# A hybrid encoder step on one core: order of the attention blocks, place of the search's state and of the MLP's low halves

## The chip, the cores and the metric

The kernel runs on one core of one Trainium2 chip. The metric is the device time of one execution in microseconds (us), lower is better. An execution of the profiler is read beside it; its span runs from the first to the last profiled instruction.

## The reference, cut to what matters

One inference step of a two-layer encoder on 1024 prompt frames and 32 sample frames, model width 1024, everything in float32. Layer 0 joins stick-breaking attention and a spatial-gating MLP. Layer 1 joins the attention below with a short gated convolution. After each mixer comes an MLP of width 4096, the same for both layers.

```python
def dsa_attend(q, qi, wi, q_pos, k, v, ki, k_pos, top_k):
    qk_idx = einsum('bqhe,bke->bqhk', qi, ki) * (D_IDX ** -0.5)
    score = einsum('bqhk,bqh->bqk', relu(qk_idx), wi) * (H_IDX ** -0.5)      # 4 index heads
    admissible = (k_pos[None, :] // CHUNK) <= (q_pos[:, None] // CHUNK)      # CHUNK = 64
    score = where(admissible, score, NEG)
    _, idx = lax.top_k(score, top_k)                                         # 256 keys, sample 136
    ...
    p = softmax(logits)                                                      # over the selected keys alone
    ...

def sq_relu_ffn(h, w1, w2):
    return jnp.square(jax.nn.relu(h @ w1)) @ w2
```

## The kernel before, in words

Activations lie transposed: features on the 128 partitions, the 1056 frames (1024 and 32) along the free dimension. Every float32 product with weights is made from three products of high and low parts (`gemm_tile`, L246 to L261): an output tile of 128 features by 1056 frames is 3 column pieces of 352 in three PSUM banks, and the jobs alternate between two such sets (banks 0 to 2 and 3 to 5, `psz`). A job waits until its set was evacuated (`set_free`) and reports on `job_done`. POOL splits each block of weights into high and low (`split`, L1676 and L1680) while PE works on the block before; SP's queue loads them.

**The MLP** (`pe_ffn`, `act_ffn`, `dve_ffn`, L274 to L357) has 16 chunks of 256 hidden features. For one chunk PE makes two up tiles (72 matmuls each, eight input tiles) and eight down tiles (18 matmuls each), and it makes the up tiles of chunk c+1 ahead of the down tiles of chunk c. For an up tile DVE evacuates with relu and scale into `rbuf` (L336), ACT squares (L316) and copies the rounded high half to `hid` (L318), DVE then makes the low half (L339) and counts `hid_ready`. For a down tile DVE adds the PSUM set to the residual `xT` (L347). DVE's order is: first tile's L336 and L339, second tile's L336 and L339, eight times L347.

**Index scores** (PE L1096 to L1112, ACT L1226 to L1233, DVE L1301 to L1316). Query blocks 2 to 7 and the sample, four index heads each, make 28 rounds. PE writes a round's scores, up to 1024 columns, into one of four pairs of banks; ACT applies relu and copies it to one of two SBUF tiles `rl`; DVE multiplies by the head's weight `wi` and accumulates in the SBUF tile `score` (L1309 for the first head, L1312 for the others). PE waits for the relu of four rounds ago, ACT for the accumulation of two rounds ago. After the 28th relu PE begins the 16 tiles of the first eight projection units of layer 1.

**The search** (L1322 to L1351, ACT's `count` L1237). The threshold of the k-th largest score of each row is found bit by bit in 32 rounds. In a round ACT counts the scores of three blocks against the candidate (L1242) and DVE those of the other four (L1340), then DVE works on tiny rows of seven columns in the SBUF tile `bs_`: two candidates for the next round (L1344, L1345), the comparison (L1348), the choice (L1350), which lets ACT go on, and the new threshold (L1351). ACT empties one of the first 12 projection tiles after two or three rounds (L1253). After the search DVE repairs the threshold and makes the mask of the selected keys (L1390 to L1397); ACT's squares of the queries (L1260) wait for that, and PE's sums over them too (L544).

**Attention over the selected keys** (PE L1140 to L1173, ACT L1264 to L1274, DVE L1423 to L1447, POOL L1482 to L1489). 36 steps: block b = step // 4, with b+1 key tiles of 128, and last the sample (b = 8, 544 keys); a step is one pair of heads. PE makes the scores (L1153); DVE scales, masks and takes the extreme (L1438); ACT takes exp with the sum (L1273); DVE the reciprocal (L1428); POOL multiplies (L1487); two steps later PE turns both matrices (L1184) into banks 4 and 5, ACT and DVE copy one each (L1287); three steps later PE multiplies with the values (L1211) into bank 6 or 7, and DVE stores the block (L1446). Beside the first 28 steps POOL runs one instruction of the short convolution each (`conv`, L1463 to L1480). The head of this stretch also has DMAs on SP's queue: copies of keys, stores of keys, values and convolution state, and the next weights.

```python
for n, (a, b) in enumerate(((0, 0), (0, 1), (1, 0))):            # L256, three products
...
ACT_BLOCKS, DVE_BLOCKS = (5, 4, 3), (2, 1, 6, 0)                 # L1064, who counts which block
...
if 0 <= it - 2 < NPAIR:                                          # L1167, PE's order in a step
    pe_p_turns(pe, 2 * (it - 2))
if 0 <= it - 3 < NPAIR:
    pe_pv(pe, it - 3)
if 0 <= it - 2 < NPAIR:
    pe_p_turns(pe, 2 * (it - 2) + 1)
```

## Time and profile before

| what | before |
|---|---|
| median of 3 runs | 2800.72 us (2800.42 to 2802.06) |
| profiled execution | 2799.82 us |
| its span | 2798.1 us |
| mean granted clock of TensorE | 0.973 |
| busy: PE, DVE, ACT, POOL | 2654.0, 1242.0, 667.4, 1166.8 us |

In the profile, PE is TensorE's matmuls and PEld its weight loads, DVE is VectorE, ACT ScalarE, POOL GpSimd, SP the engine whose queue issues most DMAs. L12 is line 12 of the kernel before. PEclk is the granted clock of TensorE as a share of full speed (1.0 is 2.4 GHz, 0.5 is 1.2 GHz). "[0.65 <-DVE xT L347]" behind an instruction says that its engine sat idle for 0.65 us before it, and that L347 on DVE ended the wait. A busy engine is not a bound by itself; what counts is what a wait was for.

### The profile page before, as it was taken

What the parts mean: (1) busy time and instruction counts of PE and PEld (TensorE: products, weight loads), DVE (VectorE), ACT (ScalarE), POOL (GpSimd) and SP (SyncE); (2) the same over time, 40 slices, a digit from 0 to 9 for tenths busy, and PEclk for the clock granted to TensorE, in tenths of its full rate; (3) what the DMA queues carried; (4) which work ended last, traced back from release to release, by engine and by line L of the source; (5) the groups of instructions that cost most, each with busy time, mean ns of one, the idle gap of its engine ahead of it and who ended that gap; (6) DMA issues with size and microseconds to landing.
All of it is one profiled execution on the core that took longest, in us unless ns stands there. A gap on an engine that the chain in (4) does not pass through costs nothing.

```text
span 2798.1 us, 38333 instructions
## 1 busy us (share of the span) xinstructions
PE 2654.0 (95%) x16253; PEld 2448.9 (88%) x16253; DVE 1242.0 (44%) x1575; ACT 667.4 (24%) x926; POOL 1166.8 (42%) x969
## 2 busy tenths in 40 slices
PE   6999999999999999999978996899999999999998
PEld 6998744699999999999965995568999999999998
DVE  5223477634333232323348998464342323232334
ACT  3200378612010101000126751354110000000000
POOL 4332366444333333334433333772433334444441
PEclk8999999999999999999999998799999999999999
DMA  5110300011111111111012110301111111111101
GB/s 189 46 46 32 114 9 1 38 57 45 45 45 45 45 45 45 45 45 45 20 66 69 45 45 15 65 2 63 46 46 45 45 45 45 45 45 45 45 30 63
DMA packets 96239, 134.02 MB, mean 48 GB/s; under 512 B 17393, under 2 KB 81969, under 8 KB 95634
## 3 DMA queue, kind: packets, MB, share of 16 engines
q1 hardware_dynamic: 92466, 114.35, 12.9%
q10 hardware_dynamic: 3680, 18.36, 1.6%
q8 instruction: 67, 1.10, 0.2%
q14 instruction: 26, 0.21, 0.0%
HBM read 113.16 MB, written 18.73 MB: 47 GB/s over the span
## 4 chain that ended last, share of the span: by engine, by line
PE 75%; DVE 12%; ACT 6%; issue 3%; POOL 2%; DMA 1%; another core or an unknown queue 0%; DVEq 0%; ACTq 0%; POOLq 0%
PE PS L259 63%; ACT reach L1242 3%; PE PS L1211 2%; PE PS L1184 2%; DVE xT L347 1%; PE PS L1153 1%; DVE rbuf L336 1%; ACT rbuf L316 1%; ACT hid L318 1%; PE PS L868 1%; PE PS L896 1%; DVE score L1312 1%; POOL spr L1015 1%; DVE reach L1340 1%; DVE sp L971 1%
## 5 line engine op out<-in xcount | busy, mean ns | idle before, releaser
L1676 POOL TENSOR_TENSOR w_sp<-stage,ones 128x512 fp32r<-128x512 f32 x372 | 391.9, 1086 | 1403.7 <-PE PS L259 1363.7
L259 PE MATMUL PS<-h,w_sp 128*128 128x352 f32 (+1 forms) x5256 | 873.4, 326 | 42.8 <-POOL w_sp L1680 14.7
L259 PEld LDWEIGHTS PS<-h,w_sp 128*128 128x128 f32 (+1 forms) x5256 | 856.1, 189 | 51.8 <-issue 25.3
L259 PE MATMUL PS<-hid,w_sp 128*128 128x352 f32 x4608 | 756.4, 324 | 19.6 <-DVE xT L347 19.6
L259 PEld LDWEIGHTS PS<-hid,w_sp 128*128 128x128 f32 x4608 | 743.4, 188 | 28.3 <-DVE xT L347 28.3
L259 PE MATMUL PS<-hz,w_sp 128*128 128x352 f32 x3456 | 567.7, 323 | 0.0
L259 PEld LDWEIGHTS PS<-hz,w_sp 128*128 128x128 f32 x3456 | 558.7, 188 | 0.0
L1680 POOL TENSOR_TENSOR w_sp<-stage,w_sp 128x512 fp32r<-128x512 f32 x372 | 526.5, 1449 | 0.0
L347 DVE TENSOR_TENSOR xT<-PS,xT 128x1056 f32<-128x1056 f32 x256 | 318.8, 1254 | 336.3 <-PE PS L259 336.3
L316 ACT ACTIVATE rbuf<-rbuf 128x1056 f32<-128x1056 f32 x64 | 69.7, 1089 | 1259.3 <-DVE rbuf L336 1259.3
L336 DVE SCALAR_TENSOR_TENSOR rbuf<-PS,rstd 128x1056 f32<-128x1056 f32 x64 | 80.5, 1257 | 505.3 <-PE PS L259 505.3
L339 DVE TENSOR_TENSOR hid<-rbuf,hid 128x1056 fp32r<-128x1056 f32 x64 | 93.5, 1461 | 145.6 <-ACT hid L318 145.6
L1242 ACT ACTIVATE reach<-score,bs__68 128x1024 bf16<-128x1024 f32 (+2 forms) x96 | 99.0, 1033 | 29.0 <-DVE bs__68 L1350 27.5
L771 DVE TENSOR_TENSOR Z<-PS,rstd 128x1056 f32<-128x1056 f32 x20 | 25.1, 1257 | 176.6 <-PE PS L259 176.6
L1015 POOL TENSOR_TENSOR spr<-sp,spr 128x1024 fp32r<-128x1024 f32 (+4 forms) x53 | 91.5, 1727 | 4.4
L1340 DVE TENSOR_SCALAR_CACHE_REDUCE reach<-score,bs__68 128x640 bf16<-128x640 f32 (+3 forms) x128 | 88.6, 745 | 2.0 <-DVE bs__68 L1351 0.4
L1013 POOL TENSOR_SCALAR spr<-sp 128x1024 fp32r<-128x1024 f32 (+4 forms) x53 | 42.0, 793 | 75.2 <-DVE sp L971 64.6
L1487 POOL TENSOR_SCALAR Lb<-Lb,st 128x128 f32<-128x128 f32 (+8 forms) x72 | 52.9, 750 | 45.6 <-DVE st L1428 45.5
L318 ACT ACTIVATE hid<-rbuf 128x1056 fp32r<-128x1056 f32 x64 | 69.6, 1088 | 2.0
L960 DVE SCALAR_TENSOR_TENSOR zs<-PS,zs 128x1024 f32<-128x1024 f32 (+4 forms) x53 | 48.0, 905 | 41.0 <-PE PS L868 40.6
L868 PE MATMUL PS<-spr,tri_r 128*128 128x512 f32 (+4 forms) x212 | 52.4, 372 | 11.0 <-POOL spr L1015 10.7
L1184 PEld LDWEIGHTS PS<-ident,Lb 128*128 128x128 f32 x288 | 31.5, 144 | 32.5 <-issue 26.9
(259 smaller groups left out, 1898.5 us busy)
## 6 DMA issues: line engine op xcount, KB each, us to landing
stage<-in_w_ffn SPq DMA_DIRECT2D x64, 1024.0 KB, 5.1
stage<-in_w_in_odd SPq DMA_DIRECT2D x10, 1024.0 KB, 4.9
stage<-in_w_in_even SPq DMA_DIRECT2D x9, 1024.0 KB, 5.0
x_spill<-xT ACTq DMA_DIRECT2D x2, 4224.0 KB, 14.0
xT<-x_spill ACTq DMA_DIRECT2D x2, 4224.0 KB, 13.5
xtok<-in_x_prompt SPq DMA_DIRECT2D x8, 512.0 KB, 7.7
stage<-in_w_out_even SPq DMA_DIRECT2D x4, 1024.0 KB, 8.9
stage<-in_w_out_odd SPq DMA_DIRECT2D x4, 1024.0 KB, 13.4
```

Source lines behind the costliest of these rows:

```text
L259: mm = pe.matmul(out[0:m, c, :], lhs, rhs(k, b)[:, c * CH:(c + 1) * CH], start=(k == 0 and n == 0), stop=(k == nk - 1 and n == 2))
L316: act.activation(x, x, ACT.Square).then_inc(s_done, 1)
L318: act.activation(hid[:, c % 2, t, 0, :], x, ACT.Copy).then_inc(hhi_done, 1)
L336: dve.scalar_tensor_tensor(tri3(rbuf[:, t, :]), psz(j + t), 0.0, tri3(rstd[:, :]), ALU.max, ALU.mult).then_inc(set_free[(j + t) % 2], 1)
L339: dve.tensor_tensor(hid[:, c % 2, t, 1, :], rbuf[:, t, :], hid[:, c % 2, t, 0, :].bitcast(F32), ALU.subtract).then_inc(hid_ready, 1)
L347: dve.tensor_tensor(tri3(xT[:, m, :]), psz(j + m), tri3(xT[:, m, :]), ALU.add).then_inc(set_free[(j + m) % 2], 1)
L1015: pool.tensor_tensor(lo, x, hi.bitcast(F32), ALU.subtract).then_inc(a_lo, 1)
L1184: mm = pe.transpose(PS[:, 4 + kt // 4, (kt % 4) * P:(kt % 4 + 1) * P], Lb[:, t % 6, kt * P:(kt + 1) * P], ident[:, :])
L1242: act.activation(reach[:, r], score[:, r], ACT.Sign, scale=-1.0, bias=bs_[:, n % 2, bi:bi + 1], accum_out=bs_[:, 2, bi:bi + 1]).then_inc(a ...
L1340: ch.mark(dve.tensor_scalar(reach[0:m, r], score[0:m, r], bs_[0:m, now, bi:bi + 1], 0.0, ALU.is_lt, ALU.add, accum_out=bs_[0:m, CNT, bi:bi ...
L1676: pool.tensor_tensor(w_sp[:, s, 0, q:q + 512], stage[:, s, q:q + 512], ones[:, 0:1].to_broadcast([P, 512]), ALU.mult).then_inc(w_hi_done, 1)
L1680: lo = pool.tensor_tensor(w_sp[:, s, 1, q:q + 512], stage[:, s, q:q + 512], w_sp[:, s, 0, q:q + 512].bitcast(F32), ALU.subtract)
```

## The change

There are four edits.

1. In the MLP, the low half of a chunk's second up tile is no longer made straight after its evacuation but after the first down tile of the chunk before it was added (`low`, `low_of`). The first up tile's low half stays, and so do both of chunk 0.
2. Attention takes its blocks in the order 7, 6, 5, 4, 3, 2, 1, 0, then the sample (`BLOCKS`). The convolution's instructions stay with the step numbers. Banks 6 and 7 go by the place in the order.
3. The index scores' relu is written back into its PSUM banks, and DVE reads them there. `rl` and ACT's wait for DVE are gone; PE waits for the accumulation of four rounds ago, and for the 27th before the projections.
4. In the search, threshold, comparison result and the bound to compare with lie in PSUM bank 7 (`state`); the candidates, UP and the counts stay in `bs_`. From the second round UP is made from the threshold by one xor with two bits. The threshold is copied back once at the end.

```diff
@@ -327,33 +327,38 @@
...
-            def up(c, dj2=0, dj=0, dt=0):
+            def low(c, t, dt=0):
+                dve.wait_ge(hhi_done, c0 + 2 * c + t + 1 + dt)
+                dve.tensor_tensor(hid[:, c % 2, t, 1, :], rbuf[:, t, :], hid[:, c % 2, t, 0, :].bitcast(F32),
+                                  ALU.subtract).then_inc(hid_ready, 1)
+
+            def up(c, dj2=0, dj=0, dt=0, last=True):
                 j = j0 if c == 0 else j0 + 2 + 10 * (c - 1)
                 for t in range(2):
-                    n = c0 + 2 * c + t
                     dve.wait_ge(job_done, j + t + 1 + dj)
...
                                              ALU.mult).then_inc(set_free[(j + t) % 2], 1)
-                    dve.wait_ge(hhi_done, n + 1 + dt)
-                    dve.tensor_tensor(hid[:, c % 2, t, 1, :], rbuf[:, t, :], hid[:, c % 2, t, 0, :].bitcast(F32),
-                                      ALU.subtract).then_inc(hid_ready, 1)
-
-            def down(c, dj2=0, dj=0):
+                    if t == 0 or last:
+                        low(c, t, dt)
+
+            def down(c, dj2=0, dj=0, dt=0, low_of=None):
...
                                       ALU.add).then_inc(set_free[(j + m) % 2], 1)
+                    if m == 0 and low_of is not None:
+                        low(low_of, 1, dt)
...
                 for c in (0, 1):
-                    up(c + 1, dj2=i * 10, dj=i * 20, dt=i * 4)
-                    down(c, dj2=i * 10, dj=i * 20)
-            up(15)
-            down(14)
+                    up(c + 1, dj2=i * 10, dj=i * 20, dt=i * 4, last=False)
+                    down(c, dj2=i * 10, dj=i * 20, dt=i * 4, low_of=c + 1)
+            up(15, last=False)
+            down(14, low_of=15)
             down(15)
@@ -1029,7 +1034,6 @@
...
         zslot = lambda name, s, shape: at(name, o_z + s * ZB, shape)
-        rl = [zslot("rl0", 9, [P, D]), zslot("rl1", 10, [P, D])]
         qiP = zslot("qiP", 16, [P, 4, NT])
@@ -1058,6 +1062,7 @@
...
         NPAIR = 36
+        BLOCKS = [7, 6, 5, 4, 3, 2, 1, 0, 8]
         ROWS = [P] * 6 + [TS]
@@ -1096,7 +1101,7 @@
...
                 if n >= 4:
-                    pe.wait_ge(i_relu, n - 3)
+                    pe.wait_ge(i_acc, n - 3)
                 b0 = 2 * (n % 4)
@@ -1109,7 +1114,7 @@
...
                 mm.then_inc(i_mm, 1)
-            pe.wait_ge(i_relu, 28)
+            pe.wait_ge(i_acc, 27)
             with pe.Fori(0, 4) as i:
@@ -1139,7 +1144,7 @@
...
                 if it < NPAIR:
-                    b, p = it // 4, it % 4
+                    b, p = BLOCKS[it // 4], it % 4
                     g = p // 2
@@ -1175,7 +1180,7 @@
...
-            b, e = t // 8, t % 2
+            b, e = BLOCKS[t // 8], t % 2
             pe.wait_ge(c_n, t + 1)
@@ -1192,12 +1197,12 @@
...
-            b, p = i // 4, i % 4
+            q, b, p = i // 4, BLOCKS[i // 4], i % 4
             g = p // 2
...
                 pe.wait_ge(c_pt[e], i + 1)
-            if p == 0 and b >= 2:
-                pe.wait_ge(c_at, b - 1)
+            if p == 0 and q >= 2:
+                pe.wait_ge(c_at, q - 1)
             n, m = (b + 1, P) if b < 8 else (5, TS)
@@ -1208,7 +1213,7 @@
...
                         w, v = w[0:TS, kt * TS:(kt + 1) * TS], vtc[0:TS, 8, g * HD:(g + 1) * HD]
-                    mm = pe.matmul(PS[64 * e:64 * e + 64, 6 + b % 2, p * P:p * P + m], v, w,
+                    mm = pe.matmul(PS[64 * e:64 * e + 64, 6 + q % 2, p * P:p * P + m], v, w,
                                    start=(kt == 0), stop=(kt == n - 1))
@@ -1226,11 +1231,8 @@
...
                 act.wait_ge(i_mm, n + 1)
-                if n >= 2:
-                    act.wait_ge(i_acc, n - 1)
-                m = ROWS[bi]
-                act.activation(rl[n % 2][0:m, 0:SCN[bi]], banks(2 * (n % 4), SCN[bi], m), ACT.Relu,
-                               scale=HD * HD ** -0.5).then_inc(i_relu, 1)
+                x = banks(2 * (n % 4), SCN[bi], ROWS[bi])
+                act.activation(x, x, ACT.Relu, scale=HD * HD ** -0.5).then_inc(i_relu, 1)
             act.wait_ge(i_acc, 28)
@@ -1265,7 +1267,7 @@
...
                 if it < NPAIR:
-                    m, n = (P, (it // 4 + 1) * P) if it < 32 else (TS, PAST + TS)
+                    m, n = (P, (BLOCKS[it // 4] + 1) * P) if it < 32 else (TS, PAST + TS)
                     for e in range(2):
@@ -1276,7 +1278,7 @@
...
-            b, e = t // 8, t % 2
+            b, e = BLOCKS[t // 8], t % 2
             x = pT[t % 4]
@@ -1303,7 +1305,7 @@
...
                 s = score[0:m, SC0[bi]:SC0[bi] + SCN[bi]]
-                x, w = rl[n % 2][0:m, 0:SCN[bi]], wi[0:m, tile, hh:hh + 1]
+                x, w = banks(2 * (n % 4), SCN[bi], m), wi[0:m, tile, hh:hh + 1]
                 dve.wait_ge(i_relu, n + 1)
@@ -1322,13 +1324,16 @@
...
             u = lambda r, a=0, b=7: bs_[:, r, a:b].bitcast(I32)
+            state = PS[:, 7, 0:64].rearrange("p (r b) -> p r b", b=8)
+            fp = lambda r: state[:, r, 0:7]
+            up_ = lambda r: state[:, r, 0:7].bitcast(I32)
             dve.wait_ge(i_acc, 28)
             ch.mark(dve.memset(f(CNT), 0.0))
-            ch.mark(dve.memset(u(THR), -1))
+            ch.mark(dve.memset(up_(THR), -1))
             for bi in range(7):
...
-                ch.mark(dve.memset(bs_[:, KV, bi:bi + 1], float(n - 2 * k + 1 if bi in ACT_BLOCKS else n - k)))
+                ch.mark(dve.memset(state[:, KV, bi:bi + 1], float(n - 2 * k + 1 if bi in ACT_BLOCKS else n - k)))
             dve.memset(u(0), 0).then_inc(cand_set, 1)
@@ -1341,14 +1346,18 @@
...
                     bit = 1 << (30 - n)
-                    ch.mark(dve.tensor_scalar(u(UP), u(now), bit, None, ALU.bitwise_xor))
-                    ch.mark(dve.tensor_scalar(u(nxt), u(THR), bit, None, ALU.bitwise_xor))
+                    if n == 0:
+                        ch.mark(dve.tensor_scalar(u(UP), u(now), bit, None, ALU.bitwise_xor))
+                    else:
+                        ch.mark(dve.tensor_scalar(u(UP), up_(THR), 3 * bit, None, ALU.bitwise_xor))
+                    ch.mark(dve.tensor_scalar(u(nxt), up_(THR), bit, None, ALU.bitwise_xor))
                 ch.sync()
                 dve.wait_ge(act_count, 3 * n + 3)
-                ch.link(dve.tensor_tensor(u(KEPT), f(CNT), f(KV), ALU.is_le))
+                ch.link(dve.tensor_tensor(up_(KEPT), f(CNT), fp(KV), ALU.is_le))
                 if n < 31:
-                    dve.copy_predicated(u(nxt), u(KEPT), u(UP)).then_inc(cand_set, 1)
-                ch.link(dve.copy_predicated(u(THR), u(KEPT), u(now)))
+                    dve.copy_predicated(u(nxt), up_(KEPT), u(UP)).then_inc(cand_set, 1)
+                ch.link(dve.copy_predicated(up_(THR), up_(KEPT), u(now)))
+            ch.link(dve.tensor_copy(u(THR), up_(THR)))
@@ -1427,7 +1436,7 @@
...
                 if it < NPAIR:
-                    b = it // 4
+                    b = BLOCKS[it // 4]
                     m, n = (P, (b + 1) * P) if b < 8 else (TS, PAST + TS)
@@ -1440,11 +1449,11 @@
...
                 if it >= 7 and it % 4 == 3:
-                    b = it // 4 - 1
-                    c0, m = tok(b)
-                    dve.wait_ge(c_pv, 4 * b + 4)
+                    q = it // 4 - 1
+                    c0, m = tok(BLOCKS[q])
+                    dve.wait_ge(c_pv, 4 * q + 4)
                     dve.tensor_copy(Z[:, OQ:OQ + 4, c0:c0 + m],
-                                    PS[:, 6 + b % 2, :].rearrange("p (k q) -> p k q", k=4)[:, :, 0:m]).then_inc(c_at, 1)
+                                    PS[:, 6 + q % 2, :].rearrange("p (k q) -> p k q", k=4)[:, :, 0:m]).then_inc(c_at, 1)
             dve_mix(dve, 4, [0, 1, 2, 3, 9, 10, 11, 12])
@@ -1480,7 +1489,7 @@
...
             for i in range(NPAIR):
-                m, n = (P, (i // 4 + 1) * P) if i < 32 else (TS, PAST + TS)
+                m, n = (P, (BLOCKS[i // 4] + 1) * P) if i < 32 else (TS, PAST + TS)
                 pool.wait_ge(c_r, i + 1)
```

## Rows read from the trace of the kernel before

**Rows 1.** The page, the chain that ended last, by engine

```profile
PE 75%; DVE 12%; ACT 6%; issue 3%; POOL 2%; DMA 1%; another core or an unknown queue 0%; DVEq 0%; ACTq 0%; POOLq 0%
```

**Rows 2.** Source L347: durations min/median/max in ns; then who waited (us, times)

```profile
L347 DVE TENSOR_TENSOR xT<-PS,xT x256: 1240/1257/1258, 695.3 to 2782.1; 128x1056 f32<-128x1056 f32 x128
...
  PE PS L259: 19.6, 30
```

**Rows 3.** Timeline 765 to 800: start, us, engine, instruction, count, [idle before]

```profile
784.47 5.83 PEld L259 LDWEIGHTS PS<-hid,w_sp 128*128 128x128 f32 x36
...
788.36 1.66 DVE L339 TENSOR_TENSOR hid<-rbuf,hid 128x1056 fp32r<-128x1056 f32 x1 [2.28 <-ACT hid L318]
...
791.25 8.95 PE L259 MATMUL PS<-hid,w_sp 128*128 128x352 f32 x54 [0.65 <-DVE xT L347]
```

**Rows 4.** Groups by shape, DVE, 1476 to 1517: busy us, mean ns, idle before

```profile
L1312 DVE SCALAR_TENSOR_TENSOR score<-rl,wi,score 128x512 f32<-128x512 f32 x3 | 4.7, 1569 | 0.3
```

**Rows 5.** Timeline of PE, 1470 to 1540

```profile
1475.87 25.60 PE L1106 MATMUL PS<-kiD,qiP 128*128 128x384 f32 x64 [1.63 <-DMA kiD<-Z]
...
1509.98 1.02 PE L1109 MATMUL PS<-kipT,qiP 128*32 128x512 f32 x2
...
1510.90 1.02 PE L1109 MATMUL PS<-kipT,qiP 128*32 128x512 f32 x2
...
1515.84 24.32 PE L259 MATMUL PS<-h,w_sp 128*128 128x352 f32 x149 [2.93 <-ACT rl L1232]
```

**Rows 6.** Timeline of DVE, three stretches of 1470 to 1664

```profile
1475.04 0.15 DVE L1299 TENSOR_SCALAR wi<-PS 128x4 f32<-128x4 f32 x1
...
1520.31 0.17 DVE L1348 TENSOR_TENSOR bs__68<-bs__68 128x7 int32<-128x7 f32 x1 [0.35 <-ACT reach L1242]
...
1524.01 0.17 DVE L1348 TENSOR_TENSOR bs__68<-bs__68 128x7 int32<-128x7 f32 x1 [0.28 <-ACT reach L1242]
...
1569.45 1.14 DVE L1348 TENSOR_TENSOR bs__68<-bs__68 128x7 int32<-128x7 f32 x1
...
1656.34 0.49 DVE L1348 TENSOR_TENSOR bs__68<-bs__68 128x7 int32<-128x7 f32 x1 [0.43 <-ACT reach L1242]
```

**Rows 7.** Waits, 1515 to 1735: us in total, times, longest us

```profile
ACT reach L1242 <- DVE bs__68 L1350: 27.5, 25, 3.0
PE PS L544 <- ACT Z L1260: 23.8, 1, 23.8
```

**Rows 8.** Stretches of attention: width, busy us by engine, PEclk, DMA share, GB/s

```profile
1774.60:1797.30 22.70, 12.22 (x55) 5.89 (x55) 6.10 (x38) 6.89 (x30) 17.85 (x20) 0.56 0.68 54
1797.30:1805.00 7.70, 7.70 (x36) 3.83 (x36) 3.41 (x13) 3.55 (x13) 3.21 (x6) 0.52 0.68 219
...
1915.00:1923.40 8.40, 6.64 (x91) 5.67 (x89) 2.29 (x11) 2.11 (x8) 1.41 (x3) 0.64 0.01 2
```

**Rows 9.** Chain of waits, 1765 to 1930: start, us, what

```profile
1787.24 9.49 another core or an unknown queue
...
1809.72 0.84 PE PS L1153 x4
...
1892.25 1.92 PE PS L1153 x8
1894.17 1.02 PE PS L1184 x8
1895.19 1.90 PE PS L1211 x32
...
1914.00 0.06 PE PS L1165 x4
```

**Rows 10.** Stretch before the scores' clock rises, columns as in rows 8

```profile
1475.00:1480.00 5.00, 4.13 (x7) 2.34 (x8) 1.47 (x6) 0.98 (x2) 1.01 (x2) 0.50 0.98 325
```

**Rows 11.** Groups by shape, POOL, 1774 to 1924: columns as in rows 4

```profile
L1475 POOL TENSOR_TENSOR yc<-yc,ytap 128x1058 f32<-128x1058 f32 x8 | 19.6, 2445 | 0.0
...
L1487 POOL TENSOR_SCALAR Lb<-Lb,st 128x256 f32<-128x256 f32 x8 | 3.8, 488 | 8.9 <-DVE st L1428 8.9
```

## The prediction

> **What bounds the kernel now.** I read the page first: of the chain that ended last, 75% is PE's [rows 1]. So only two kinds of edit can pay: one that lets PE start a stretch earlier, or one that removes a gap of PE. The views by line and the timelines then say where such gaps are, near the four places that the change touches.
>
> The MLP: the source view of L347 says that PE waited 30 times, 19.6 us in all, for the DVE's addition L347 [rows 2]. The timeline of one chunk shows why [rows 3]: the up tile ends near 784.7, L336 evacuates it, then DVE sits waiting for ACT's hi half (2.28 us) and makes the low half L339 (1.66), and only then adds the first two down tiles, which by then fill both PSUM sets. PE restarts at 791.25 after 0.65 us.
>
> The index scores (1476 to 1516 us): DVE is busy almost throughout. Its L1312 takes 1569 ns for 512 columns [rows 4], though L347 does more than twice as many in 1257: something other than length slows it, and it has two inputs in SBUF. PE sends its pairs of banks and then starts the projections at 1515.84, when the last relu is done [rows 5].
>
> The search (1517 to 1657): its small DVE instructions take 0.17 us, or 1.14 for the same shape at another time [rows 6]; ACT waited 27.5 us for them [rows 7]. But the projections run on PE meanwhile without a gap, and later PE waits 23.8 us for the first squares after the selection [rows 7]. So what ends this stretch is index, search and selection in series; PE has slack in it.
>
> Attention (1774.6 to 1923.4, 148.8 us): the window view [rows 8] shows its phases. In the first 22.7 us PE is busy 12.22 at a granted clock of 0.56, with a hole of 9.49 us [rows 9] while the DMA engines are 0.68 busy; then 7.7 us fully busy at 0.52; then it works without a gap until the sample's steps; and in the last 8.4 us it is busy 6.64 at 0.64.
>
> **The MLP's low halves.** Moved: for every chunk but the first of each MLP, the second L339 comes after the first L347. Nothing is added; 30 places. New order on DVE after an up tile at time 0, with the durations of [rows 3]: evacuation to 1.3, first down tile ready at 2.95 (18 matmuls; the loads of 36 take 5.83), its addition to 4.2, low half to 5.9 at the worst shown duration, second down tile ready at 5.9, its addition to 7.2. PE's third down tile needs the first addition at 5.9 (has it at 4.2), its fourth the second one at 8.85 (has it at 7.2). ACT's hi half is ready at 3.6, before the DVE asks for it, so the moved wait holds up nothing behind it. PE needs the low half only one whole chunk later. Cover if all this is wrong: 1.6 us of slack. Gain: all of 30 x 0.65 = **19.6 us** [rows 2].
>
> **The index scores.** ACT's relu stays in PSUM, DVE reads its first input there, PE waits for the DVE (four heads back) instead of for ACT. A PSUM and an SBUF input together is the form of L347: 1240 to 1258 ns for 1056 columns over 256 instances, although POOL works beside many of them [rows 2]. That is 0.157 + n/960 us: 0.69 for 512, 1.22 for 1024, plus 0.09 between two. Then PE is the slowest: a head of the sample, 512 and 32 columns, goes out every 0.92 us [rows 5], so 1024 columns take some 1.71 and 512 some 0.86. Four heads each of 512 to 1024 take 3.4, 4.3, 5.1, 6.0, 6.8, the sample 3.7, and the 384 ones 5.1, twice their share, because the clock is at 0.50 there [rows 10]. Sum 34.4: PE ends at 1475.87 + 34.4 = 1510.3. The next-to-last relu and addition follow, so the projections start at 1511.1 instead of 1515.84 and the search 4.8 earlier. **Gain 4.8.** The relu's write into PSUM is in no row; at 1.03 (today) or at 1.71 it hides behind PE. If POOL delayed the DVE as today the gain would be nothing: bounds 0 and 4.8. I take the upper since that very form is in [rows 2].
>
> **The search.** State rows move to PSUM, one copy back is added (0.15), UP is computed from THR. With no slow instances the search would run ahead, but ACT empties one projection tile after every two or three rounds, and the tiles come at PE's pace (72 matmuls at 0.162 [rows 3]: 11.64 us). The last three rounds follow the eleventh tile: 1511.1 + 11 x 11.64 + 1.1 = 1640.2, plus 10.5 us for three rounds (3.70 from one L1348 to the next [rows 6], less the last step), ends at 1650.8 against 1656.3. So beyond the 4.8 that all shifts, only 0.8 is left, less 0.2 for the copy, less the fix-up instructions that now meet more of POOL's split. **I take 0.4**; bounds -2 and +2, since the selection after it, unchanged, meets POOL's work at other points.
> A PSUM input at this size took 0.15 us, SBUF 0.17 for a near size [rows 6]. By the Trainium skill (VectorE: DVE Perf Modes, the section on the TRN2 errata) the fixed part of a DVE instruction is 120 cycles from PSUM and 58 from SBUF, an estimated 0.065 us more for each; the trace does not show it, and by it the last three rounds would be some 0.4 us longer, a total of 2776.3.
>
> **Attention from the longest block.** The work is the same, so I count PE's time by step (one of 36). Scores, two turns and products take 1.92 + 2 x 1.02 + 1.90 = 5.86 us in block 7, and the scores 0.84 in block 2 [rows 9]; every part falls by some 0.216 per block, so a step costs 5.21, 4.56, 3.91, 3.26, 2.61, 1.96, 1.31 for blocks 6 to 0, and the 32 steps 114.7. *Start:* at half clock the first three score steps take 3.84 each with the two DVE passes (1.22 each, by the law above) exposed, about 1.6 us between: PE is at 14.7 us after the two, the turns of step 0 and ACT's copy take it to 20.3, the fourth scores to 22.2. It then has 4 x 1.92 + 2.04 = 9.7 of 114.7 behind it, and full clock, as PE has been nearly dense for 8 us. *Middle:* 105.0 more, of which 2.2 (the last turns and products of block 0) lie inside the sample's steps. POOL has in block 1 two normalisations of 0.49 and a convolution of at most 2.44 [rows 11], so between 1.0 and 3.4 a step; for the first seven steps of today it was busy 17.85 less 2.7 for the end of cinp, 2.2 a step [rows 8]. I take 2.5, over PE's 1.96: +1.5 with the overlap at its ends (no convolution comes after step 27). In block 0 the exp, reciprocal and copy chain, not PE, sets the step: +2. *Tail:* the sample's steps have no long block beside them: 2.7 each (scores 1.1, then two DVE passes), 9.4 in all, then the drain of today, 9.4 (the last scores end at 1914.06 [rows 9]). Sum 22.2 + 102.8 + 3.5 + 18.8 = 147.3, or 149.5 if the clock falls in the tail a little earlier than today. Today 148.8. **I take 0**, bounds -2.5 and +1. The hole of 9.49 us is counted as not repeated: in it PE stood still with little in its queue behind it; now the same 22 us pass in filling the pipe with long steps. SP's and POOL's DMAs do not move.
>
> **Sum.** 19.6 + 4.8 + 0.4 + 0 = 24.8 us. The profiled execution took 2799.82, 1.7 over its span and 0.9 under the median 2800.72; from the median, **2776**. A change under 0.2% (5.6 us) could not be told from none.
>
> **Rivals.**
> *The hole stays* (0.22). It begins 12.7 us after the start of attention and ends at 22.1, whatever PE does. For: the DMA engines are busy then whatever the order [rows 8]. Against: it began at one place of PE's stream, which would now be reached later. PE then has three score steps done, not four and a turn: 4.0 us, and 3.9 more at the lower clock after it. 2776 + 8 = 2784.
> *The tail costs less and the clock rises sooner* (0.14): low clock ends 5 us sooner and block 0 is bound by PE: -6, 2770.
> *The low half is late* (0.07): POOL delays L339 at its new place; it is then done after 7.6 and PE waits 0.3 us in each chunk: +9, 2785.
> *PSUM does not shield the DVE* (0.05): index and search keep their times: +5, 2781.
> *Slower than before* (0.02): long steps first leave gaps in PE during the fill, and the granted clock stays at 1.2 GHz as in 1774 to 1805 [rows 8]. Each step of block 7 then costs 5.86 more. It passes the old time from 25 us, a little over four such steps; if blocks 7 to 5 run so, 62.6 us are added: 2839.
> The forecast itself has 0.5. Its own range is 2771 to 2781.
>
> **How the numbers follow.** The range reaches from the early-clock case to beyond the hole: 2768 to 2787. It leaves out the last rival and some extremes of the MLP's. Faster 0.96, within 0.2% 0.02, slower 0.02: the 19.6 us alone are over three times the bound.
>
> **What would show it.** L347 should have no PE behind it in the MLP, and ten down and up tiles should take 46.7 us, not 47.3. L1312 should take 0.69 for 512 columns and 1.22 for 1024; the projections start 35.2 us after the first index matmul, not 40.0. The small instructions of the search should have no instance over 0.3 us, and ACT should wait for PE's tiles in it. From the first attention matmul to the last should stay within 146 to 150 us; at 156 the hole is back. I am wrong if the attention moves by more than 3 us either way, or if the MLP returns less than 17.

## The result, and the profile after

The kernel after took 2767.63 us (median of 4 runs, 2766.34 to 2768.53), the kernel before, run beside it, 2801.12 (4 runs, 2800.42 to 2802.06). The ratio is 0.9882, with an interval of 0.9867 to 0.9897: 33.5 us faster, where 24.8 was forecast. The median lies 8.4 us under the forecast and 0.4 under the lower end of the range. Between the two profiled executions the gain is 31.3 us of span; the other 2.2 come from where each stands among its own runs (before's is 1.3 below its median, after's 0.9 above).

Page of the kernel after, the chain that ended last, by engine. To be held against [rows 1]:

```profile
PE 87%; DVE 7%; POOL 2%; issue 2%; ACT 1%; DMA 1%; SPq 0%; POOLq 0%; DVEq 0%; ACTq 0%
```

PE's share went from 75 to 87%: most of the waits for DVE and ACT that used to be in the chain are gone from it (DVE 12 to 7%, ACT 6 to 1%). To see where, I took the time of the same instruction in both traces, from the start of the span, and subtracted. The shift grows in these steps: +1.8 before the first MLP (nothing was changed there; over fourteen traces that MLP begins anywhere from 689.9 to 694.7), -13.5 over that MLP, -3.3 from the first index matmul to the first count of the search, -0.2 over search and selection, -0.8 to the start of attention, -2.0 over attention, +0.2 over the output projection, -13.5 from there to the end. Sum -31.3.

**The MLP.** Source view of L350 in the kernel after (the addition that was L347), durations min/median/max in ns, then who waited for it, us and times:

```profile
L350 DVE TENSOR_TENSOR xT<-PS,xT x256: 1243/1258/1258, 694.9 to 2750.8; 128x1056 f32<-128x1056 f32 x128
...
who waited for it (us, times):
  ACT sq L460: 36.7, 8
  PE PS L1813: 1.4, 1
```

Timeline of PE and of DVE in one chunk of the kernel after:

```profile
784.62 23.42 PE L259 MATMUL PS<-hid,w_sp 128*128 128x352 f32 x144
...
784.82 1.26 DVE L340 SCALAR_TENSOR_TENSOR rbuf<-PS,rstd 128x1056 f32<-128x1056 f32 x1 [6.79 <-PE PS L259]
787.73 1.26 DVE L350 TENSOR_TENSOR xT<-PS,xT 128x1056 f32<-128x1056 f32 x1 [1.65 <-PE PS L259]
788.90 2.37 DVE L332 TENSOR_TENSOR hid<-rbuf,hid 128x1056 fp32r<-128x1056 f32 x1
791.20 1.24 DVE L350 TENSOR_TENSOR xT<-PS,xT 128x1056 f32<-128x1056 f32 x1
...
831.25 1.26 DVE L340 SCALAR_TENSOR_TENSOR rbuf<-PS,rstd 128x1056 f32<-128x1056 f32 x1 [6.79 <-PE PS L259]
```

All 144 down matmuls run as one piece of 23.42 us, where [rows 3] had a break at 791.25. The first down tile's addition comes at once and the low half after it. The chunk, from one L340 to the next, takes 831.25 - 784.82 = 46.43 us. Before, it took 832.13 - 784.82 = 47.31: 0.88 less, and 13.5 us over the whole MLP are 0.90 for each of its 15 waits, not 0.65. Where the difference hides is seen in the kernel before, in two rows that I had not used: the weight loads of the same chunk, and in the source view of L347 who waited for it.

```profile
791.24 8.82 PEld L259 LDWEIGHTS PS<-hid,w_sp 128*128 128x128 f32 x55 [0.94 <-DVE xT L347]
...
  PEld PS L259: 28.3, 30
  PE PS L259: 19.6, 30
```

The same 30 waits stand there twice. The weight load waited 0.94 us each time, the matmul 0.65, and the chunk became shorter by nearly the former.

**The index scores.** Groups by shape, DVE, 1464 to 1502 (busy us, mean ns, idle before), then the timeline of PE:

```profile
L1314 DVE SCALAR_TENSOR_TENSOR score<-PS,wi,score 128x1024 f32<-128x1024 f32 x3 | 3.8, 1282 | 1.2 <-ACT PS L1235 1.2
...
L1314 DVE SCALAR_TENSOR_TENSOR score<-PS,wi,score 128x512 f32<-128x512 f32 x3 | 2.3, 751 | 0.3
```

```profile
1464.16 31.36 PE L1111 MATMUL PS<-kiD,qiP 128*128 128x384 f32 x80 [1.88 <-DMA kiD<-Z]
...
1499.10 0.22 PE L1115 MATMUL PS<-kiD,qiP 128*32 128x32 f32 x2
1500.96 9.31 PE L259 MATMUL PS<-h,w_sp 128*128 128x352 f32 x56 [1.64 <-DVE score L1314]
```

For 512 columns 751 ns stand against the 1569 of [rows 4]. The projections start 36.8 us after the first index matmul, 39.97 before [rows 5]. What ends the stretch now is the DVE, which still adds the sample's heads when PE is done.

**The search.** Groups by shape, DVE, 1502 to 1645, then two of the waits of 1500 to 1720 (us in total, times, longest):

```profile
L1356 DVE TENSOR_TENSOR PS<-bs__68,PS 128x7 int32<-128x7 f32 x32 | 5.5, 170 | 29.6 <-ACT reach L1244 29.6
L1358 DVE COPY_PREDICATED bs__68<-PS,bs__68 128x7 int32<-128x7 int32 x31 | 5.3, 170 | 1.1
L1359 DVE COPY_PREDICATED PS<-PS,bs__68 128x7 int32<-128x7 int32 x32 | 5.3, 164 | 0.0
```

```profile
PE PS L549 <- ACT Z L1262: 23.4, 1, 23.4
...
ACT Z L1255 <- PE PS L259: 15.9, 5, 3.8
```

No instance is slow any more (before, the same group as L1356 had a mean of 411 ns), but the time went over to other waits: ACT now waits 15.9 us for PE's tiles, which it never did before, and DVE 29.6 for ACT, where it was 8.0.

**Attention.** Windows of the kernel after, columns as in [rows 8], then PE's timeline of the start:

```profile
1758.50:1773.50 15.00, 10.06 (x32) 3.98 (x32) 6.78 (x13) 4.77 (x8) 9.95 (x8) 0.77 0.55 82
1773.50:1788.50 15.00, 12.89 (x123) 9.31 (x124) 7.75 (x15) 9.57 (x15) 8.34 (x7) 1.00 0.84 126
```

```profile
1758.53 1.99 PE L1158 MATMUL PS<-Z 64*128 64x512 f32 x8 [1.02 <-DVE kpTc L1431]
1762.97 3.57 PE L1158 MATMUL PS<-Z 64*128 64x512 f32 x8 [2.46 <-DVE st L1447]
1769.00 2.78 PE L1158 MATMUL PS<-Z 64*128 64x512 f32 x8 [2.46 <-DVE st L1447]
```

The DMA engines are no less busy than before in the second window (0.84), and PE works through it: the hole of [rows 9] is not repeated. In its place stand two waits of 2.46 us at the start, and near the end two for POOL, of 0.93 and 1.40 us. Behind these two the granted clock is at 0.50 from 1884 to 1888, in the short steps of the last prompt block, and again from 1900 to the end of attention; the kernel before has full clock there until about 1917, less than 7 us before its end.

### The profile page after: what moved, and what is told of

The parts are those of the page before. It is cut to its first block, busy times and chain, and to the rows that moved or that the text cites. A ratio compares the mean times of both kernels' runs of the same rounds, so it can differ in the third digit from the quotient of the medians.

```text
span 2766.8 us, 38308 instructions
## 1 busy us (share of the span) xinstructions
PE 2642.9 (96%) x16253; PEld 2449.1 (89%) x16253; DVE 1229.0 (44%) x1576; ACT 667.9 (24%) x926; POOL 1158.8 (42%) x969
## 4 chain that ended last, share of the span: by engine, by line
PE 87%; DVE 7%; POOL 2%; issue 2%; ACT 1%; DMA 1%; SPq 0%; POOLq 0%; DVEq 0%; ACTq 0%
PE PS L259 74%; PE PS L1189 1%; PE PS L1216 1%; PE PS L1158 1%; PE PS L1111 1%; PE PS L901 1%; PE PS L873 1%; POOL spr L1020 1%; DVE sp L976 1%; PE PS L549 1%; DVE sp L970 1%; PE PS L889 1%; PE PS L475 1%; PE PS L572 1%; DVE Z L1403 0%
## 5 line engine op out<-in xcount | busy, mean ns | idle before, releaser
L350 DVE TENSOR_TENSOR xT<-PS,xT 128x1056 f32<-128x1056 f32 x256 | 321.5, 1256 | 358.5 <-PE PS L259 358.5
L340 DVE SCALAR_TENSOR_TENSOR rbuf<-PS,rstd 128x1056 f32<-128x1056 f32 x64 | 80.5, 1257 | 505.4 <-PE PS L259 505.3
L332 DVE TENSOR_TENSOR hid<-rbuf,hid 128x1056 fp32r<-128x1056 f32 x64 | 112.1, 1752 | 77.3 <-ACT hid L318 77.3
L1244 ACT ACTIVATE reach<-score,bs__68 128x1024 bf16<-128x1024 f32 (+2 forms) x96 | 99.0, 1032 | 12.3 <-DVE bs__68 L1358 10.2
L1496 POOL TENSOR_SCALAR Lb<-Lb,st 128x1024 f32<-128x1024 f32 (+8 forms) x72 | 52.7, 746 | 42.9 <-DVE st L1437 42.8
L1275 ACT ACTIVATE Lb<-Lb,st 128x1024 f32<-128x1024 f32 (+8 forms) x72 | 54.6, 762 | 21.1 <-DVE st L1447 21.0
```

The source lines that it names most:

```text
L332: dve.tensor_tensor(hid[:, c % 2, t, 1, :], rbuf[:, t, :], hid[:, c % 2, t, 0, :].bitcast(F32), ALU.subtract).then_inc(hid_ready, 1)
L340: dve.scalar_tensor_tensor(tri3(rbuf[:, t, :]), psz(j + t), 0.0, tri3(rstd[:, :]), ALU.max, ALU.mult).then_inc(set_free[(j + t) % 2], 1)
L350: dve.tensor_tensor(tri3(xT[:, m, :]), psz(j + m), tri3(xT[:, m, :]), ALU.add).then_inc(set_free[(j + m) % 2], 1)
L1244: act.activation(reach[:, r], score[:, r], ACT.Sign, scale=-1.0, bias=bs_[:, n % 2, bi:bi + 1], accum_out=bs_[:, 2, bi:bi + 1]).then_inc(a ...
```

## The experiments

The table gives, of each kernel's profiled execution, the us between the same two instructions: first MLP (first hidden matmul to the sums of the second norm), index (first index matmul to first projection), search with selection (first count to the sample's mask), and attention (first scores to last evacuation). Each kernel has one trace. The medians of the second column were taken in four groups, and the kernel before, measured in each, had 2801.12 (beside the kernel after), 2798.80 (the four single edits), 2800.07 (stores later or left out), 2800.58 and 2800.80 (the last four rows); so gains are read from the ratios, not down this column. "Stop" is every idle time over 1 us in attention that the trace puts down to "remote", an unknown queue, with the engine that stood still (a part of it can be a plain wait).

| kernel | median | MLP | index | search | attention | stop |
|---|---|---|---|---|---|---|
| before | 2801.12 | 710.00 | 39.97 | 207.60 | 149.07 | ACT 9.89, DVE 3.86 |
| after | 2767.63 | 696.48 | 36.80 | 207.38 | 147.09 | none |
| MLP edit alone | 2774.40 | 696.48 | 39.82 | 209.15 | 150.10 | ACT 9.08, DVE 4.50, 2.26 |
| order alone | 2799.23 | 709.94 | 39.93 | 207.78 | 148.87 | DVE 3.42 |
| index edit alone | 2796.27 | 710.00 | 36.38 | 207.79 | 148.23 | DVE 5.51, 2.29, 1.83 |
| state in PSUM alone | 2801.13 | 710.00 | 39.83 | 207.17 | 149.97 | ACT 9.75, DVE 3.18, 2.62 |
| before, stores later | 2800.26 | 709.98 | 39.73 | 210.43 | 148.45 | DVE 5.78 |
| before, no stores | 2790.79 | 709.99 | 39.90 | 209.23 | 140.66 | none |
| after, old order, stores later | 2767.60 | 696.48 | 36.23 | 207.36 | 148.75 | ACT 7.19 |
| after, stores later | 2774.35 | 696.47 | 36.35 | 207.40 | 155.71 | DVE 9.75 |
| after, old order, stores in rows | 2763.54 | 696.47 | 36.70 | 207.38 | 142.29 | none |
| after, stores in rows | 2768.68 | 696.48 | 36.40 | 207.36 | 147.67 | none |
| after, low half one addition later | 2766.94 | 696.48 | 36.38 | 207.36 | 147.64 | none |
| after, old order, stores in rows turned earlier | 2761.11 | 696.48 | 36.34 | 207.37 | 141.85 | none |

### The MLP edit alone

```
+                    if m == 0 and low_of is not None:
+                        low(low_of, 1, dt)
```

> Only the MLP edit on the kernel before. Theory A (a restart of PE costs what the weight loads show, 0.94 us each, since matmul ends are modelled): 28 us faster, some 2773, and a chunk takes 46.4 us instead of 47.35. Theory B (it costs the 0.65 us of the matmul row, as the prediction had it): 20 us faster, 2781, and a chunk takes 46.7.

It took 2774.4 us, a ratio of 0.991 with an interval of 0.9895 to 0.9926, some 24 to 25 us faster than the 2798.8 of the kernel before beside it. Its two MLPs gave back 13.5 us each, 27.0 in all (0.90 for each of the 30 waits), as in the kernel after. The rest of the kernel was 1 us longer than in before's trace, in parts that it leaves unchanged. So the weight load's idle time comes near the price of such a wait (theory A), and the matmul's 19.6 us does not.

### The block order alone

```
+        BLOCKS = [7, 6, 5, 4, 3, 2, 1, 0, 8]
...
-                    b, p = it // 4, it % 4
+                    b, p = BLOCKS[it // 4], it % 4
```

> Only the order of the attention blocks on the kernel before. Theory A (filling the pipe with long steps costs what the hole cost, and the hole does not come back): first attention matmul to last evacuation 147 us instead of 149.1, total 2 us faster. Theory B (the order itself is a gain, the other edits hid part of it): 5 us or more faster. Rival: the hole of 9.5 us is back beside long blocks, 6 to 8 us slower.

2799.23 us, ratio 0.9998 (0.9989 to 1.0007): no difference. Its attention is as long as before's, 148.87 against 149.07, although of the stop only 3.42 us are left. So none of the three came out as written: attention is not 2 us shorter, nothing is gained, and the hole is not back in full.

### The index edit alone

```
-                act.activation(rl[n % 2][0:m, 0:SCN[bi]], banks(2 * (n % 4), SCN[bi], m), ACT.Relu,
-                               scale=HD * HD ** -0.5).then_inc(i_relu, 1)
...
+                act.activation(x, x, ACT.Relu, scale=HD * HD ** -0.5).then_inc(i_relu, 1)
```

> Only the index scores in PSUM on the kernel before. Theory: the projections start 36.8 us after the first index matmul instead of 40.0, and all that follows moves with them: 3 us faster. Rival: with the search's state still in SBUF its slow instances hold the search up, and the 3 us are lost again before the selection: under 1 us.

2796.27 us, ratio 0.9989 (0.998 to 0.9999): faster by about 3 us, though the interval reaches from 0.3 to 5.6. The search is 207.79 us, no longer than before's by more than 0.2, so nothing was lost in it. The stretch itself is 3.6 us shorter than before's. So the edit gives 3.2 to 3.6 us, in the eight traces that have it 3.2 to 3.7, and not 4.8.

### The search's state in PSUM alone

```
-                    ch.mark(dve.tensor_scalar(u(nxt), u(THR), bit, None, ALU.bitwise_xor))
+                    ch.mark(dve.tensor_scalar(u(nxt), up_(THR), bit, None, ALU.bitwise_xor))
```

> Only the search's state in PSUM on the kernel before. Theory: ACT's waits for the small DVE instructions fall from 27.5 to about 10 us, but the last rounds wait for PE's projection tiles, so the search ends 0 to 1 us earlier and the total is the same within 1 us. Rival: the 17 us of slow instances come back as time, up to 17 us faster.

2801.13 us, ratio 1.0006 (0.9997 to 1.0016): no difference in the total. ACT waits 10.2 us for the small DVE instructions, as the theory had it. The table shows something a single pair could not: the eight traces with the state in PSUM lie between 207.17 and 207.40 us, the six with it in SBUF between 207.60 and 210.43, with a mean of 208.7. The edit removes a scatter. Against the profiled execution of before it is worth 0.2 us, against the mean of such executions 1.3.

### Is it the small stores?

The hole of [rows 9] needed a cause. Timeline of the kernel before at the end of the hole, ACT, DVE and PE; in brackets what ended the idle time:

```profile
1792.99 0.42 DVE L1438 CUSTOM_DVE_ANT_0 Lb<-PS,m 128x256 f32<-128x256 f32 x1 [3.86 <-remote]
1793.34 0.08 DVE L1438 DVE_READ_ACCUMULATOR2_ANT st<- 128x1 f32 x1
1796.76 0.38 ACT L1287 ACTIVATE pT<-PS 128x256 f32<-128x256 f32 x1 [9.89 <-remote]
...
1797.26 0.29 PEld L1184 LDWEIGHTS PS<-ident,Lb 128*128 128x128 f32 x2 [7.96 <-issue]
```

ACT stands for 9.89 us before a copy whose input PE had finished turning at 1789.1, so 7.7 of them have no engine behind them; DVE stops for 3.86 between the two halves of a pair of scores that PE had given by 1787.8. Then PE waits for both. What had been issued shortly before: the four stores of the convolution's state, written as 2048 packets of 4 bytes, ahead of two weight loads. The trace has the small packets at 2.2 to 5.6 us after the start of attention, and the weights behind them until 28.7; ACT's stop is from 12.3 to 22.2. First they were moved behind the weights and behind the fifth attention block, in the kernel before, then left out (their outputs are not written):

```
+            for n in range(2, 4):
+                weights(U_OOUT + n, cols(dram["w_out_odd"][0])[:, :, n * 256:(n + 1) * 256])
+            sp_.wait_ge(c_at, 5)
...
             for name, c in (("prompt", TP), ("sample", NT + 2)):
```

> The kernel before, with the four stores of the convolution state (2048 packets of 4 bytes) issued behind the last weights of the output projection and after the fifth block of attention, not near its start. Theory (these stores clog the DMA engines, and that makes the hole of 9.5 us): no hole, attention 149.1 to about 139 us, total 8 to 10 us faster. Rival (the hole has to do with PE's place in its stream alone): hole and time as before. Second rival (the stores stop PE wherever they run): the hole moves into the middle, time as before.

> The kernel before without the four stores of the convolution state, which are left out. Theory: no hole, attention some 139 us. Rival: the hole is there without them.

Later stores: 2800.26 us, ratio 0.9998 (0.9988 to 1.0008), attention 148.45. The first hole was gone; DVE stood still for 5.78 us once the stores had run, and the granted clock fell to a mean of 0.62 in the 8 us behind it: the second rival. No stores: 2790.79 us in a single run, attention 140.66, no stop. So the stores cost 8 us or so in the kernel before, early or late.

The same shift in the changed kernel, with the old order and with the new:

> The changed kernel with attention in the old order (shortest block first) and the stores of the convolution state late. Theory: the short first steps fill the pipe in a third of the time and no hole stops them; attention 139 us against 147 in the changed kernel, total 2760. Rival: the long blocks last leave a slower tail and it is 2766 or more.

> The changed kernel with the stores of the convolution state late. Theory (in the changed order the stores cost nothing, since there was no hole): 2767 within 1.5. Rival (part of the slow fill was the stores): 3 us or more faster.

With the old order 2767.6 us (ratio 0.9879, 0.9862 to 0.9895), ACT stopped for 7.19. With the new order 2774.35 (0.9902, 0.9886 to 0.9919), 6.7 us slower than the kernel after. Both theories fell, each by about 7 us, and in both cases there is a stop that they had ruled out; the first rival's "2766 or more" was met, but by the stop and not by a slower tail. Timeline and chain of waits of the latter, around the stop:

```profile
1883.19 0.42 DVE L1289 COPY pT<-PS 128x256 f32<-128x256 f32 x1 [9.75 <-remote]
...
1883.73 0.29 PEld L1189 LDWEIGHTS PS<-ident,Lb 128*128 128x128 f32 x2 [9.52 <-issue]
```

```profile
1873.44 9.73 another core or an unknown queue
```

and the DMA queues of 1860 to 1900 in it (packets, MB, share of 16 engines):

```profile
q1 hardware_dynamic: 2112, 0.01, 2.6%
q8 instruction: 2, 0.03, 0.4%
q14 instruction: 3, 0.02, 0.4%
```

The small packets are recorded at 109.3 to 111.3 us of attention. DVE stands still from 116.0 to 125.7, and all others behind it, with no data packet on its way. In the two other kernels with later stores the stop also begins only when the last of the small packets is over, by 4.5 and 7.7 us. The load of w_out_odd, long done, is no part of it, nor is the bandwidth.

### Stores of rows

The same values leave as 16 packets of 512 bytes: TensorE turns the four columns, ScalarE copies them out.

```
+            for n, c in enumerate((TP, TP + 1, NT + 2, NT + 3)):
+                mm = pe.transpose(PS[0:4, 7, n * P:(n + 1) * P], cinp[:, :, c], ident[:, :])
+            mm.then_inc(cv_tp, 1)
...
+            act.activation(pT[0][0:4, 0:512], PS[0:4, 7, :], ACT.Copy).then_inc(cv_rd, 1)
...
+                sp_.dma_start(dram["new_d_conv_" + name][0, 0].rearrange("j (k p) -> k j p", p=P),
+                              pT[0][0:4, v * 256:(v + 1) * 256].rearrange("k (j p) -> k j p", p=P)).then_inc(cv_out, 16)
```

> The kernel after with the old block order, and the four conv-state stores (2048 packets of 4 bytes) replaced: TensorE turns the same values into 4 rows behind the last attention block, ScalarE copies them out, two stores of 8 packets of 512 bytes leave then. Theory A (the many small packets hold up an engine's supply in attention; the order edit cured that hole and by itself costs): attention about 140.7 us as in the run without the stores, against 147.1 in the kernel after, so 2767.6 - 6.4 = about 2761 us, up to 2762 with the turning. Theory B (the order edit is worth its time for another reason, and the stores' place is all that counts): no shorter than the kernel after, 2767 or more.

> The kernel after, new block order kept, with the same turned stores. Theory A: the new order has no hole left to take away, so attention stays at 147 us and the kernel at 2766 to 2768 us, some 6 us behind the version with the old order. Theory B (the new order still pays for the packets somewhere): several us under the kernel after, level with the old order's version.

Old order 2763.54 us (ratio 0.9866, 0.985 to 0.9883), attention 142.29; new order 2768.68 (0.9885, 0.9869 to 0.9902), attention 147.67. Theory A held for both in the main: no stop in either, the old order gains and the new one has nothing to gain; but the old order's attention is 1.6 us longer and its total 1.5 to 2.5 longer than expected. So the new order by itself costs 5 to 6 us (147.7 against 142.3), and in the kernel after it pays because no stop falls into it. The rows leave at 143.6 us or later, behind attention, where no small packets were ever sent; so these two runs show what it is worth to have the small stores out of attention, and not whether 16 packets in its midst would be harmless or 2048 behind it.

The turning delayed the output projection by 1.1 us, so it was put where TensorE waits for others:

```
+                if it == NPAIR + 1:
+                    pe.wait_ge(cv_done, 3)
+                    pe.wait_ge(c_at, 8)
```

> The version with the old order and the turned stores, but TensorE turns the four columns before the second last pair's turns of the sample block, where it waits for other engines, and ScalarE copies them out while it waits for the last values. In the version before, the output projection began 3.64 us after the last evacuation, against 2.55 in the kernel after: 1.1 us is to come back if the turning is covered (theory A), so about 2762.4 us, 5 us under the kernel after. Rival: TensorE's 1.02 us lands on the chain of the sample block's pairs and the gain is given back: 2763 to 2764.

2761.11 us (4 runs, 2760.04 to 2762.32; ratio 0.9858, 0.9841 to 0.9874): 6.5 under the kernel after, the fastest of all. The rows leave at 138.4 us here, 3.4 before attention ends. Timeline of PE and ACT in it:

```profile
1894.37 1.01 PE L1152 MATMUL PS<-ident,cinp 128*4 128x128 f32 x4
...
1896.29 0.57 ACT L1286 ACTIVATE pT<-PS 4x512 f32<-4x512 f32 x1
...
1900.32 3.03 ACT L509 ACTIVATE h<-Z 128x1056 fp32r<-128x1056 f32 x3 [3.47 <-DVE Z L1465]
```

The copy is done 3.47 us before ACT is wanted again, and the projection follows the last evacuation by 2.56 us, as in the kernel after.

### The low half one addition later

```
-                    if m == 0 and low_of is not None:
+                    if m == 1 and low_of is not None:
```

> The kernel after with the second low half of the MLP one add later (behind the second of the eight adds, not the first). Theory A (its cover is nearly used: in the kernel after it ends at 791.27 and the second add at 792.44, about 1 us ahead of the matmul that reads it): the low half ends 1.2 to 2.4 us later or some 0.2 to 1.3 us late in each of 30 chunks, 5 to 35 us slower than the kernel after. Rival (anything behind the second relu is early enough): level with the kernel after, within 2 us.

2766.94 us (two runs), level with the kernel after; theory A fell. Timeline of DVE in it:

```profile
787.46 1.26 DVE L350 TENSOR_TENSOR xT<-PS,xT 128x1056 f32<-128x1056 f32 x1 [1.65 <-PE PS L259]
790.37 1.26 DVE L350 TENSOR_TENSOR xT<-PS,xT 128x1056 f32<-128x1056 f32 x1 [1.65 <-PE PS L259]
791.54 1.95 DVE L332 TENSOR_TENSOR hid<-rbuf,hid 128x1056 fp32r<-128x1056 f32 x1
793.41 1.24 DVE L350 TENSOR_TENSOR xT<-PS,xT 128x1056 f32<-128x1056 f32 x1
```

Counted from L340 the low half ends 8.94 us later, against 6.45 in the kernel after, and nobody waits for it. The expectation had given it a reader at the second addition; the sentence of the prediction, that PE needs it only one chunk later, was the right one.

## Why the prediction was right or wrong

**The MLP, 19.6 us forecast, 27.0 measured.** The mechanism was right: the reordered additions, their times within 0.6 us, and no new wait. The step that failed is the size of the term, "30 x 0.65". The trace had two idle times for each wait. I took the matmul's, but the records of a long row of matmuls end later than the loads that feed them, as the profile's page says of their modelled ends, and so hid 0.29 us of every gap; the loads' 0.94 is what the MLP gave back (0.90). This one term is 7.4 us. The other three come to 0.3 together (-1.5, -0.2, +2.0), stretches that the forecast left out to -1.2, and the place of the two profiled executions among their runs to 2.2, less 0.4 since the kernel before was that much slower this time: some 8.4 in all.

**The index scores, 4.8 forecast, 3.3 measured.** PSUM did shield the DVE, so the rival that it would not is out. The law "0.157 + n/960" from a two-dimensional PSUM operand of 1056 columns gave 0.69 for 512, and 0.751 was measured, 1.282 in place of 1.22 for 1024; and I let only one relu and one addition follow PE's end, while DVE still had three of 0.84 us in line. PE's end came 35.2 us after its start against 34.4, the projections 1.6 later than forecast. By the Trainium skill (SBUF — State Buffer, Who interferes with whom) a DVE instruction with two SBUF inputs contends with GpSimd's reads and one with a PSUM input does not. These traces agree: 1569 against 751 ns here, and up to 2369 ns for L332, which keeps two SBUF inputs, against at most 1258 for L350 with one in PSUM, both of 128x1056, and POOL's splits run beside many of both.

**The search, 0.4 forecast, 0.2 measured.** Right, and for the reason given: ACT waits for PE's tiles (15.9 us). The rule of the Trainium skill that was weighed there (VectorE: DVE Perf Modes, TRN2 errata) foresaw a longer instruction from PSUM; 0.143 to 0.171 us with PSUM operands against 0.15 to 0.17 without [rows 6] do not show it. What I missed is that with the state in SBUF the time varied by 2.8 us.

**Attention, 0 forecast, 2.0 measured, bounds -2.5 and +1.** Read as a change of the time, the bounds hold the -2.0. The prediction's own sum had given 147.3, 1.5 less than today's, of which it took nothing. That sum, against 147.1 measured, came out right by luck, through errors that cancel: the fourth scores ended 19.3 us after the start, not 22.2, since the granted clock was at 0.77 in the first 15 us and not at a half; from there to the last scores it took 118.4 and not 115.7, of which POOL's 0.93 and 1.40 and the clock of 0.50 behind them are a part; the drain took 9.4, as forecast. That the hole goes was argued from a picture of queued work, which the runs don't bear out as a rule: the order alone still had a stop of 3.42 us, and the order with later stores one of 9.75. "Hole stays" was a sounder rival than its price made it.

**The other rivals.** Slower, the low half late and the unshielded DVE did not occur. Of "the clock rises sooner" the first half came true, and the steps after it gave it back.

## What to carry to other kernels

Where a matmul and its weight load show different idle times before the same wait, price the wait from the load's, and check it by the period of the loop: a chunk's length needs no model. Before a reorder is credited with a gap that it removes, find what makes the gap. Here the new order shortened attention by 2.0 us in the kernel after and by nothing alone; taking the 2048 packets of 4 bytes out of attention, in the old order, shortened it by 7.2. An edit that shows no gain against one trace may still remove scatter, which only a row of traces shows.

## What the runs showed of the hardware

Small stores can stop a compute engine. Of ten traces with the 2048 packets inside attention eight have a stop of 2 to 10 us of an engine that waited for no other; of the four without them none has. It is not always the same engine (ACT four times, DVE in seven), and it follows the stores by 4.5 us or more: with early stores it begins at 12 to 22 us into attention, with later ones at 84, 88 and 116. The two traces with early stores and no stop are of the kernel after and of its twin with the low half one addition later.

Small stores also hold up the loads behind them. In the kernel before the 2048 packets of w_out_odd, 1024 bytes each, take from 6.0 to 28.7 us of attention; with the small stores moved behind them they take from 2.8 to 10.5. Two views of the same stretch, 1789 to 1799.5, of the kernel before and of the one without stores, show how busy the DMA engines still are in the one and how idle in the other:

```profile
q1 hardware_dynamic: 711, 0.72, 81.4%
```

```profile
q8 instruction: 1, 0.02, 0.7%
q14 instruction: 1, 0.01, 0.3%
```

This backlog alone does not make the stop: the kernel after has it (until 30.3 us) and no stop, and in the three kernels with later stores the stop comes without it.

What stops the engine stays open. A candidate is the engines' supply of instructions, which comes by DMA too: without the stores one instruction packet of queue q14 came 17.45 us after the start of attention and one of q8 at 21.86, with them at 26.80 and 28.42. But the times speak against its plain form. In all eight traces with a stop the next instruction packet is recorded only after the engine had resumed, by 1.3 to 5.5 us (in the kernel before ACT resumed at 22.2, in the one with the old order and later stores at 90.8 with the packet at 96.0), and no instruction packet starts within a stop. Late packets may thus follow from a stop and not cause it. And in the kernel after a packet of q8 came some 7 us later than in the runs without that backlog, and no engine stopped. Not tried: the small packets spread thinly, the same packets behind attention, and 16 packets of rows in its midst.
